# Compressed keys and values: from slab-stationary products with a bias column to window-stationary products with two turns

## The reference, cut to what matters

```python
def compress(kv, pe, w1, w2):              # kv: [B, 512, 2 groups, 64]
    chunks = kv.reshape(B, n_chunks, CMP_STRIDE, G, dh)        # 32 chunks of 16 tokens
    blocks = jnp.concatenate([chunks[:, i:i + nc] for i in range(r)], axis=2)   # r = 2, nc = 31
    blocks = blocks + pe[None, None, :, None, :]
    flat = blocks.transpose(0, 3, 1, 2, 4).reshape(B, G, nc, CMP_LEN * dh)      # 31 x 2048
    return jax.nn.silu(flat @ w1) @ w2     # w1: 2048 x 256, w2: 256 x 64

z = h @ w_in                               # the projection that gives kv, queries, gates ...
kc = compress(kv_groups(zkc), pe_ck, w_ck1, w_ck2)
vc = compress(kv_groups(zvc), pe_cv, w_cv1, w_cv2)
o_nsa = nsa_attention(q_nsa, kc, vc, k_s, v_s, k_w, v_w, nsa_gates)
```

## Time and profile before

| | |
|---|---|
| median of 3 runs | 2798.16 us (2796.82 to 2799.88) |
| the profiled execution's own time | 2794.6 us |
| its span, first to last instruction | 2792.4 us |
| TensorE busy | 2158.1 us (77%), 6380 passes |
| VectorE busy | 1745.0 us (62%) |
| ScalarE busy | 756.3 us (27%) |
| GpSimd busy | 626.2 us (22%) |
| mean granted clock of TensorE | 0.872 |

### The profile page before, as it was taken

How to read it: one execution, slowest core, us unless ns; L and a number is a source line. 1 busy time by engine, 2 the same in 40 slices (tenths; PEclk the granted TensorE clock), 3 DMA queues, 4 the chain that set the end, 5 groups by cost and what they waited for, 6 DMA issues and landing times.

```text
span 2792.4 us, 20560 instructions
## 1 busy us (share of the span) xinstructions
PE 2158.1 (77%) x6380; PEld 1024.5 (37%) x6380; DVE 1745.0 (62%) x3714; ACT 756.3 (27%) x2109; POOL 626.2 (22%) x540
## 2 busy tenths in 40 slices
PE   5999999999999999999899555555555555555564
PEld 3474544444444444444468321112111221112121
DVE  5424465310114314224659999999999999989987
ACT  2012343110000002222332333333333333333332
POOL 0000000000000000000014444444444444444453
PEclk9989999999999999999999777777777777777767
DMA  9520101112136421211049999999999999999997
GB/s 367 229 91 31 61 31 61 61 61 90 63 147 244 183 85 61 90 61 61 17 185 371 386 415 413 416 386 422 421 418 396 414 414 411 421 391 414 416 416 329
DMA packets 85496, 694.56 MB, mean 249 GB/s; under 512 B 9488, under 2 KB 9488, under 8 KB 10512
## 3 DMA queue, kind: packets, MB, share of 16 engines
q0 software_dynamic: 77184, 587.24, 51.7%
q1 hardware_dynamic: 7200, 98.57, 9.2%
q10 hardware_dynamic: 1008, 7.52, 0.7%
HBM read 691.19 MB, written 2.10 MB: 248 GB/s over the span
## 4 chain that ended last, share of the span: by engine, by line
PE 47%; DMA 23%; DVE 20%; issue 6%; POOL 3%; ACT 1%; POOLq 0%; DVEq 0%; ACTq 0%
PE PS L447 21%; DMA arena<-in_peer_uv,arena 17%; PE PS L477 8%; DVE arena L1777 6%; DMA ring<-in_peer_uv,arena 5%; PE PS L982 4%; DVE arena L1765 3%; PE PS L1028 3%; DVE ring L1765 3%; POOL arena L1849 2%; PE PS L632 2%; PE PS L652 1%; PE PS L641 1%; PE PS L1003 1%; PE PS L1160 1%
## 5 line engine op out<-in xcount | busy, mean ns | idle before, releaser
L1313 PE MATMUL PS<-ring,arena 128*128 128x512 f32 x472 | 363.4, 915 | 372.1 <-ACT arena L1467 342.4
L1849 POOL DMA_INDIRECT arena<-in_peer_uv,arena x276 | 335.0, 1214 | 810.6 <-DVE arena L1747 463.2
L1313 PE MATMUL PS<-arena 128*128 128x512 f32 x480 | 314.2, 793 | 174.1 <-ACT arena L1467 173.7
L447 PE MATMUL PS<-arena,ring 128*128 128x512 f32 x832 | 372.1, 606 | 9.1 <-DVE arena L1556 4.8
L1765 DVE CUSTOM_DVE_ANT_0 arena<-arena 128x1024 f32<-128x1024 f32 x276 | 334.7, 1227 | 59.0 <-DMA arena<-in_peer_uv,arena 57.8
L1849 POOL DMA_INDIRECT ring<-in_peer_uv,arena x236 | 278.1, 1178 | 369.1 <-DVE arena L1777 282.3
L1313 PEld LDWEIGHTS PS<-ring,arena 128*128 128x128 f32 x472 | 117.5, 274 | 598.5 <-ACT arena L1467 497.9
L1460 ACT ACTIVATE arena<-arena 128x1 f32<-128x1 f32 x512 | 103.0, 201 | 827.4 <-DVE arena L1765 826.8
L1765 DVE CUSTOM_DVE_ANT_0 ring<-ring,arena 128x1024 f32<-128x1024 f32 x236 | 283.2, 1222 | 55.1 <-DMA ring<-in_peer_uv,arena 51.0
L447 PE MATMUL PS<-hT,ring 128*128 128x256 f32 (+1 forms) x944 | 311.7, 491 | 5.8 <-ACT hT L337 3.6
L1313 PEld LDWEIGHTS PS<-arena 128*128 128x128 f32 x480 | 112.0, 250 | 378.1 <-ACT arena L1467 266.7
(11 more groups left out here) (287 smaller groups left out, 2398.2 us busy)
## 6 DMA issues: line engine op xcount, KB each, us to landing
ring<-in_wstream SPq DMA_DIRECT2D x46, 2048.0 KB, 7.4
arena<-in_ada POOLq DMA_DIRECT2D x24, 2048.0 KB, 8.3
arena<-in_peer_uv,arena POOLq DMA_INDIRECT x276, 9.7
ring<-in_peer_uv,arena POOLq DMA_INDIRECT x236, 9.6
xT<-in_xT ACTq DMA_DIRECT2D x1, 2048.0 KB, 13.6
arena<-in_alibi ACTq DMA_DIRECT2D x1, 2048.0 KB, 12.3
result<-arena SPq DMA_DIRECT2D x4, 512.0 KB, 8.4
arena<-in_subkeys ACTq DMA_DIRECT2D x1, 1024.0 KB, 4.9
```

The lines of the kernel that those rows point to most:

```text
L447: ins = pe.matmul(o, l, r, start=(a == 0), stop=(a == len(lhs) - 1))
L1313: ins = pe.matmul(bank(6 + b), diag[:, k % NDIAG, :], rows[slot_of(n)][:, D + b * 512:D + (b + 1) * 512], start=opens, stop=closes)
L1849: pool.indirect_dma_start(rows[j], None, ap["peer_uv"], bass.IndirectOffsetOnAxis(ap=eidx[:, t, e:e + 1], axis=0)).then_inc(landed[j], 16)
```

## The change

The operands of the first layer change sides. VectorE now adds the position term itself and writes the windows out, token pair by token pair, as `win[r]` of 16 x 62 columns (L1538 of the new file, eight TENSOR_TENSOR of 8 x 31 elements that read the stack at a step of 16 words). The 62 columns are the stationary operand and the slab's 256 hidden columns the moving one, so the hidden layer comes out window by hidden unit: keys on partitions 0 to 61, values on 64 to 125. Both streams stand one behind the other on TensorE. SiLU needs no bias. Its result is turned by two transposes for each of keys and values, copied by VectorE, and then multiplied by `ck2` and `cv2` as before. The third group, the memsets, the bias column and its copies are gone. `hid` gets a sibling `hidv` for the values.

```diff
-        stk = [area(108, 3, S), area(114, 3, S)]
+        stk = [area(108, 2, S), area(112, 2, S)]
+        win = [area(100, 16, 2, NC), area(104, 16, 2, NC)]
+        hsil = area(96, 256)
+        hidv = area(97, 124)
...
@@ TensorE @@
                 w = ring[n % 2][:, :].rearrange("p (l m) -> p l m", l=16)
-                if r == 0:
-                    pe.wait_ge(c_stk, 10)
-                for hc in range(2):
-                    for l in range(16):
-                        rhs = stk[r][:, :, 2 * l:2 * l + 16 * (NC - 1) + 1:16]
-                        ins = pe.matmul(PS[:, 2 * r + hc, 0:3 * NC].rearrange("p (g j) -> p g j", g=3), w[:, l, tile(hc)],
-                                        rhs, start=(l == 0), stop=(l == 15))
-                ins.then_inc(mm_done, 1)
-                pe.wait_ge(c_hid, 2 * r + 2)
-                (ck2 for r == 0, cv2 for r == 1)
+                pe.wait_ge(c_win, 2 * r + 2)
+                for l in range(16):
+                    ins = pe.matmul(PS[64 * r:64 * r + 62, 2 + r, 0:256], win[r][:, l, :, :].rearrange("p g j -> p (g j)"), w[:, l, :],
+                                    start=(l == 0), stop=(l == 15))
+                ins.then_inc(mm_done, 1)
+            for r in range(2):
+                q = slice(64 * r, 64 * r + 62)
+                pe.wait_ge(c_hid, r + 1)
+                for hc in range(2):
+                    ins = pe.transpose(PS[:, 4 + r, 62 * hc:62 * hc + 62], hsil[q, tile(hc)], ident[q, q])
+                ins.then_inc(c_turn, 1)
+            pe.wait_ge(c_copy, 1)
+            (ck2 from hid)
+            pe.wait_ge(c_copy, 2)
+            (cv2 from hidv)
@@ ScalarE @@
             for r in range(2):
-                act.wait_ge(c_pe, 1 + r)
-                act.wait_ge(c_mm, r) if r else None
-                for hc in range(2):
-                    act.activation(hid[:, hc * 62:(hc + 1) * 62], PS[:, 2 * r + hc, 0:2 * NC], ACT.Silu,
-                                   bias=hb[:, hc:hc + 1]).then_inc(c_hid, 1)
+                q = slice(64 * r, 64 * r + 62)
+                act.wait_ge(mm_done, MM0["ck"] + r + 1)
+                act.activation(hsil[q, :], PS[q, 2 + r, 0:256], ACT.Silu).then_inc(c_hid, 1)
@@ VectorE, projection stage, after the four copies of stk[r] @@
-                own(dve.memset(stk[r][:, 2, :], 0.0))
-                dve.tensor_copy(stk[r][:, 2, 0:32:2], prow("pek" if r == 0 else "pev")).then_inc(c_stk, 1)
+                dve.wait_ge(c_stk, 4 * r + 4)
+                for a in range(2):
+                    tok = stk[r].rearrange("p g (j s) -> p g j s", s=16)[:, :, a:a + NC, 0:16:2]
+                    pos = prow("pek" if r == 0 else "pev", 8 * a, 8 * a + 8)
+                    for g in range(NG):
+                        ins = dve.tensor_tensor(win[r][:, 8 * a:8 * a + 8, g, :], tok[:, g, :, :].rearrange("p j b -> p b j"),
+                                                pos.unsqueeze(2).to_broadcast([P, 8, NC]), ALU.add)
+                    ins.then_inc(c_win, 1)
@@ VectorE, compression stage @@
             for r in range(2):
-                dve.wait_ge(mm_done, MM0["ck"] + r + 1)
-                if r:
-                    dve.wait_ge(c_hid, 2)
-                dve.tensor_copy(hb, PS[:, 2 * r:2 * r + 2, 2 * NC]).then_inc(c_pe, 1)
-                dve.wait_ge(c_mm, r + 1)
-                (copy to kcT for r == 0, to vcm for r == 1)
+                dve.wait_ge(c_turn, r + 1)
+                dve.tensor_copy(hid if r == 0 else hidv, PS[:, 4 + r, 0:124]).then_inc(c_copy, 1)
+            (copy to kcT after c_mm 1, to vcm after c_mm 2)
```

More of the change, by code:

```diff
@@ L252, in build @@
         hid = small(0, 124)
-        hb = small(124, 2)
         kcT = small(126, NC)
@@ L1073, in build @@
         g_sig, g_turn = sem("gates_sigmoid"), sem("gates_turned")
-        c_stk, c_mm, c_pe, c_hid, c_out = (sem(n) for n in ("cmp_stacked", "cmp_hidden", "cmp_bias", "cmp_silu", "cmp_out"))
+        c_stk, c_win, c_hid, c_turn, c_copy, c_mm = (
+            sem(n) for n in ("cmp_stacked", "cmp_windows", "cmp_silu", "cmp_turned", "cmp_copied", "cmp_out"))
         y_tmp = sem("y_tmp")
@@ L1162, in _ @@
-                ins.then_inc(mm_done, 1)
-                pe.wait_ge(c_hid, 2 * r + 2)
-                if r == 0:
-                    for g in range(NG):
-                        for hc in range(2):
-                            ins = pe.matmul(PS[g * DH:(g + 1) * DH, 0, 128:128 + NC], prow("ck2", hc * DH, (hc + 1) * DH),
-                                            hid[:, hc * 62 + g * NC:hc * 62 + (g + 1) * NC], start=(hc == 0), stop=(hc == 1))
-                    ins.then_inc(c_mm, 1)
-                else:
-                    for g in range(NG):
-                        for hc in range(2):
-                            ins = pe.matmul(PS[0:NC, 1, 128 + g * DH:128 + (g + 1) * DH],
-                                            hid[:, hc * 62 + g * NC:hc * 62 + (g + 1) * NC],
-                                            prow("cv2", hc * DH, (hc + 1) * DH), start=(hc == 0), stop=(hc == 1))
-                    ins.then_inc(c_mm, 1)
+                pe.wait_ge(c_win, 2 * r + 2)
@@ new lines, in _ @@
+            pe.wait_ge(c_copy, 1)
+            for g in range(NG):
+                for hc in range(2):
+                    ins = pe.matmul(PS[g * DH:(g + 1) * DH, 0, 128:128 + NC], prow("ck2", hc * DH, (hc + 1) * DH),
+                                    hid[:, hc * 62 + g * NC:hc * 62 + (g + 1) * NC], start=(hc == 0), stop=(hc == 1))
+            ins.then_inc(c_mm, 1)
+            pe.wait_ge(c_copy, 2)
+            for g in range(NG):
+                for hc in range(2):
+                    ins = pe.matmul(PS[0:NC, 1, 128 + g * DH:128 + (g + 1) * DH],
+                                    hidv[:, hc * 62 + g * NC:hc * 62 + (g + 1) * NC],
+                                    prow("cv2", hc * DH, (hc + 1) * DH), start=(hc == 0), stop=(hc == 1))
@@ L1536, in _ @@
             for r in range(2):
-                dve.wait_ge(mm_done, MM0["ck"] + r + 1)
-                if r:
-                    dve.wait_ge(c_hid, 2)
-                dve.tensor_copy(hb, PS[:, 2 * r:2 * r + 2, 2 * NC]).then_inc(c_pe, 1)
-                dve.wait_ge(c_mm, r + 1)
-                if r == 0:
-                    own(dve.tensor_copy(kcT, PS[:, 0, 128:128 + NC]))
-                else:
-                    own(dve.tensor_copy(vcm[0:NC, :], PS[0:NC, 1, 128:256]))
+                dve.wait_ge(c_turn, r + 1)
+                dve.tensor_copy(hid if r == 0 else hidv, PS[:, 4 + r, 0:124]).then_inc(c_copy, 1)
+            dve.wait_ge(c_mm, 1)
+            own(dve.tensor_copy(kcT, PS[:, 0, 128:128 + NC]))
+            dve.wait_ge(c_mm, 2)
+            own(dve.tensor_copy(vcm[0:NC, :], PS[0:NC, 1, 128:256]))
             fence(dve, "dve")
```

2 lines of the change are left out of this document (1 added, 1 removed).

## The result

The changed kernel takes 2780.97 us (median of 5 runs, 2780.82 to 2784.74); the kernel before took 2796.82 in the same comparison (5 runs, 2792.87 to 2799.88). The ratio is 0.9949, with the interval 0.9934 to 0.9963: faster by 0.5%. The profiled execution took 2783.46 us (span 2781.2), 11.1 less than the one of before.

What follows compares the result with a forecast made beforehand. The prediction took the serial compression stage, with its second stream at half clock, as the bound at the change. Terms +0.8 - 12.9 + 0.5 = -11.6 us gave a median of 2786.6 us, range 2783.5 to 2795.5.

Steps and rivals of the forecast that it cites:

- Streams, -12.9: Both compression streams on TensorE, with the hand-over between them: 27.2 us becomes 14.3 at full clock, -12.9 us.
- The tie with the slab's load: Value slab lands just as the first stream ends its issue: 0.1 us of wait, 5 us as far end.
- The prediction's reason for the clock: TensorE's clock fell to 0.50 in the nearly idle hand-over between the streams; without it, 1.00 holds through both.
- VectorE's preparation, +0.8: VectorE's window building before the streams ends the projection 0.8 us later, bounds 0.1 and 2.7.
- the cover of 1.4 us: Slack before TensorE's spread of the query norm: 1.4 us of VectorE's added preparation costs nothing.
- the outer bound: VectorE's stepped reads at twice the element cost: 2.0 us on top; projection's end shifts by 2.7 us at most.
- Tail, +0.5: From the streams' end to the attention's first matmul: 2.8 us against 2.32, +0.5 us (0.2 to 0.9).
- After the tail: Attention's start: clock falls behind the second stream, 3.8 us at 0.50 as before; counted unchanged, with +-2 us.
- Rival A: Clock falls within the streams, array too narrowly filled or value slab late: -4.6 us, 2793.6 us; chance 0.17.
- Rival B: Stepped VectorE reads delay the spread, clock falls before the streams, narrow streams cannot raise it: +6 us, 2804; chance 0.08.
- Rival C: Gain partly given back, slab 1 to 3 us late or fill paying 2 us more: -8.5 us, 2789.7; chance 0.10.

Runs made afterwards that it cites:

- plain_read: Changed kernel with VectorE's eight TENSOR_TENSOR reading the stack contiguously, so the windows hold other tokens; 2776.76 us (1 run).
- late_windows: Changed kernel with VectorE's stack copies and windows for the values moved behind the query norm and the fence; 2778.75 us, ratio 0.9942.
- order_only: Kernel before with its old operands, but both streams back to back and both second layers behind them; 2782.85 us, ratio 0.9956.
- handover: Changed kernel with the old order: turns and second layer of the keys stand between the streams again; 2782.52 us, ratio 0.9952.
- late_slab: Changed kernel with the load of the values' slab issued later, behind the keys' fourth matmul; 2782.42 us, ratio 0.9962.
- again: The changed kernel measured and profiled once more, with nothing changed; 2778.75 us, ratio 0.9941.
- warm: split with two spare matmuls of the identity in TensorE's waits of the tail; 2775.59 us, ratio 0.9923.
- narrow: Changed kernel with 31 instead of 62 stationary columns in 14 of the 16 matmuls of each stream; 2780.07 us (2 runs), ratio 0.9950.
- slow_tail: Changed kernel with a square-root activation ahead of the values' SiLU, forcing further table loads; 2783.93 us, ratio 0.9960.
- split: late_windows with the values' stream on two halves of the array's width, VectorE adding the sums, keys' second layer first; 2778.04 us, ratio 0.9944.
- split_again: split measured and profiled once more, unchanged, beside warm; 2778.97 us, ratio 0.9940.

## Why the prediction was right, and where it was wrong

*Streams, -12.9: right.* Measured -13.1. Passes come 0.22 us apart and the clock is 1.00. The tie with the slab's load, priced at 0.1 us, came about as well: between the streams the weight loads (PEld) of the kernel after wait for it, though no gap shows between its passes. From TensorE's waits, 178.2 to 179.8 us (total, times, longest):

```profile
PEld PS L1159 <- DMA ring<-in_wstream: 0.4, 1, 0.4
```

In the other profiles with this tie it is 0.2 to 0.5 us (plain_read, late_windows), with streams of 13.95 and 14.28 us, so some 0.2 us of the 14.15 may be this wait. By order_only and handover, the order takes the hand-over's 2.9 us out of the path, and the exchange of operands shortens the streams from 20.7 us to 14.15. The prediction's reason for the clock, that it had fallen because of the idle hand-over, is not borne out as a rule: in handover TensorE was as idle (busy 0.55 of 2.80 us, against 0.58 of the 2.77 from 180.24 to 183.01 before) and the clock stayed at 1.00. That it would hold through the new streams was right all the same; it fell in them only in late_slab.

*VectorE's preparation, +0.8: right in the sum, half wrong in the working.* Measured +0.94; the cover of 1.4 us was right (the statistics are 2.4 us later, 158.57 - 151.06 against 154.88 - 149.79). But the spacing was taken at 0.34 to 0.42 us and is 0.49, inside the outer bound that the prediction kept for a stepped read. plain_read puts all of the excess down to the step: at 0.33 the cover was enough. The Trainium skill's page "SBUF — State Buffer", section "Door 1: The DMA port swizzle", had spoken for this: accesses that cross 16-byte lines are penalised. Taken with the factor of TensorE's rows, 1.5, it gave the right spacing ratio (0.49 / 0.33); put on the whole 0.42 us, as in the prediction, it gave a shift of 2.5, which is too much, because the plain spacing is 0.33. The two waits for the stacks, 0.17 us each in the sum, do not show either: the first addition starts 0.46 us behind the last copy's start, as the copies do behind one another (0.45).

*Tail, +0.5: over-sized.* Measured 0.0. SiLU took 0.38 us (0.47 taken), the second layer of the keys 0.43 (0.60), that of the values 0.64 (0.85): each price had come from a row that was at half clock or of another shape, and I had leaned to its high side.

*"After the tail", counted unchanged: the step that failed.* The prediction let the clock fall somewhere behind the second stream and stay low in the fill for as long as in the earlier trace rows, "the same, with +-2 us". Two things are wrong there. The attention's first scores, 1.85 us, were at half clock before and are 1.01 in after and in again; that 0.84 was never in the sum. And the fill's share, up to the second unit's scores, is not the same: 5.58 us before, 5.28 in again, where the clock falls for 3.4 us, 3.63 in after, where it holds. The term is -2.8 in the profile after and -1.1 in again. With the tail's 0.5 it is what separates -11.6 from the local -14.9. The forecast had carried the price over from a stretch that was at half clock from its first instruction; now the clock is at 1.00 there, and either holds or falls a little later. Of the -2.8, 1.1 came in both profiles; the other 1.7 hangs on where the clock happened to hold in this one and is luck. With again's local -13.4 the forecast's own base, 2798.16, would have led to 2784.8, inside the range.

*Further on.* 1.3 us came from outside the stage: behind a wait of TensorE for VectorE of 3.54 us the clock fell before and did not after. Timeline and stretch, before:

```profile
403.35 6.96 PE L447 MATMUL PS<-arena,ring 128*128 128x512 f32 x12 [3.54 <-DVE arena L1556]
```

```profile
403.40:406.50 3.10, 3.10 (x4) 1.45 (x5) 2.67 (x4) 2.32 (x5) 0.00 (x0) 0.50 0.00 0
```

and after:

```profile
389.69 8.63 PE L449 MATMUL PS<-arena,ring 128*128 128x512 f32 x18 [3.54 <-DVE arena L1561]
```

```profile
389.70:392.80 3.10, 3.06 (x7) 1.27 (x8) 2.95 (x5) 2.37 (x5) 0.00 (x0) 1.00 0.00 0
```

But the unchanged kernel lost the clock at the same place in again:

```profile
390.98 6.82 PE L449 MATMUL PS<-arena,ring 128*128 128x512 f32 x12 [3.54 <-DVE arena L1561]
```

```profile
391.00:394.10 3.10, 3.10 (x4) 1.41 (x5) 2.70 (x4) 2.36 (x5) 0.00 (x0) 0.54 0.00 0
```

The wait is 3.54 us in all thirteen profiles; the clock held behind it in three (after, warm, plain_read) and fell in ten. So these 1.3 us are no effect of the change. Up to the first gather the kernel after gains 16.3 us in its first profile and 13.7 in again.

*The median.* 2786.6 was reckoned from 2798.16. The kernel before itself measured 2796.82 beside the kernel after, which is 1.3 of the 5.6 us missed; the clock and the tail are 3.3, the fall at 403 us 1.3. These add up to 5.9, of which 3.0 (1.7 at the fill, 1.3 near 400 us) are missing in again, whose median is no higher; and the expert stage varies by more than what is left. So the sum is a reading of one profile, not a proof, and where the medians' further gain comes from stays open.

*Rival A* (clock falls within the streams): its first reason is refuted by narrow. Its second, the slab, by late_slab: with 2.33 us of waiting the clock does fall, for 3.4 us and not for the rest of the stream; A's price of 7.0 would have been 1.7 and the wait. *Rival B* (slower) needed narrow streams that cannot raise the clock; in late_slab it rose under them. The overrun stayed under 1 us. *Rival C*: not seen; the slab came late by a few tenths of a us, not by 1 to 3. What the Trainium skill's page "TensorE: Matmul & The Clock Gate", section "Part 1: The HAM clock gate", says of the gate, that it follows how busy the engine is, came out right for the new streams; the old one, busy for 13.97 of 14.0 us at 0.50, still speaks against it as the only rule.

*Open.* What decides in one and the same program whether the clock falls behind the tail: after (held) and again (fell) differ in no instruction. The Trainium skill's page and section just named call the gate's windows free-running, so that where a transition falls varies from run to run; that would fit, but no run here shows it. It fell in six of the eleven profiles besides after (again, slow_tail, late_windows, split, split_again, narrow) and held in the other five. Nor is it settled why handover's idle 2.8 us kept the clock when the old one lost it: the kernel before was profiled once, and whether its second stream runs at half clock in every execution is not known. The -14.9, -12.0 and -9.7 all count from that one profile. And no interval separates the kernels of the table from one another, except warm's, which stands apart from those of slow_tail, late_slab, handover and order_only.

## What to carry to other kernels

Put matmul streams that feed separate consumers back to back and do their small second halves behind both: here the order alone gave 9.7 us, the exchange of operands alone 12.0, and both 14.9, so test each by itself before giving the gain to one. When a change moves where TensorE's clock stands, price the work that follows at the clock that it will find, instruction by instruction, rather than carry the old time over. And profile the same program more than once: the clock alone moved 3 us between two profiles of it. Where a stationary operand fills half the array's width or less, try its passes on the two halves in turn; split saved 3.6 us of stream and paid 1.2 for adding the halves. Count VectorE's fp32 reads at a step of 64 bytes at 1.5 times the contiguous ones.

## What the runs showed of the hardware

- In a stream of 256-column passes on 62 stationary columns the clock rose from 0.50 to 1.00 about 3.4 us after it fell (late_slab); in a stream of 93-column passes on 128 stationary columns it stayed at 0.50 for 14 us, yet the same passes ran at 1.00 for 20.7 us (order_only). One profile each.
- With 31 stationary columns the clock stayed at 1.00 as with 62, at 0.22 us a pass (narrow).
- Passes that alternate between the two halves of the array's columns overlap: 32 in 3.67 us instead of 7.1 (split).
- VectorE's fp32 TENSOR_TENSOR of 248 elements: 412 ns contiguous, 569 ns with one operand at a step of 64 bytes.
- The same idle time does not always bring the clock down: 2.8 us in the hand-over did before and did not in handover; 3.54 us near 400 us did in ten profiles and did not in three, and of the one unchanged program it did in again and not in after.
